# Square sums of the differential blocks moved out of the attention stage into the gate stage behind it

## The reference

```python
h, gate = _modulate(x, c, norm_g, w_ada, b_ada)
qa, ka, va, qb, kb, vb, g = _split(h @ w_in, EVEN_SPLITS)
...
ya = _window_gqa_sink(qa, ka, va, kac, vac, a_sink)
...
yb = _sweep_query_blocks(lambda n, qn: _diff_attend(qn, kb_all, vb_all, lam), qb)
yb = rmsnorm(yb, b_subln_g) * (1.0 - lam_init)
y = jnp.concatenate([ya.reshape(B, S, -1), yb.reshape(B, S, -1)], axis=-1) * jax.nn.silu(g)
x = x + gate * (y @ w_out)
```

## Time and profile before

| | |
|---|---|
| median of three runs | 2830.58 us (2827.45 to 2832.51) |
| the profiled execution | 2830.81 us, of which its span 2829.0 us |
| PE busy | 2726.1 us, 96% |
| DVE busy | 1069.9 us, 38% |
| ACT busy | 785.7 us, 28% |
| POOL busy | 223.7 us, 8% |
| differential stage | about 560 to 770 us |
| gate stages | about 769 to 917 us |

### The profile page before, as it was taken

How to read it: one execution, slowest core, us unless ns; L and a number is a source line. 1 busy time by engine, 2 the same in 40 slices (tenths; PEclk the granted TensorE clock), 3 DMA queues, 4 the chain that set the end, 5 groups by cost and what they waited for, 6 DMA issues and landing times. The chain is left out here.

```text
span 2829.0 us, 32445 instructions
## 1 busy us (share of the span) xinstructions
PE 2726.1 (96%) x12154; PEld 1529.1 (54%) x12154; DVE 1069.9 (38%) x3023; ACT 785.7 (28%) x1684; POOL 223.7 (8%) x409
## 2 busy tenths in 40 slices
PE   5999999999999999999999999999999999999998
PEld 3477544477644445466745476444654465644443
DVE  3257521299712223344400174123833473212211
ACT  3136400277711112322200264112211462111100
POOL 2000000000000000000060030200000002012000
PEclk8999999999999999999999999999999999999999
DMA  7030000012011220211010001333220204134311
GB/s 261 7 109 32 20 30 30 30 68 72 34 65 65 79 86 19 93 38 38 12 54 30 30 22 42 86 83 119 96 71 30 71 16 133 67 119 168 133 60 45
DMA packets 71867, 188.46 MB, mean 67 GB/s; under 512 B 6844, under 2 KB 9600, under 8 KB 70784
## 3 DMA queue, kind: packets, MB, share of 16 engines
q0 software_dynamic: 27808, 99.04, 10.8%
q1 hardware_dynamic: 43152, 86.97, 8.9%
q10 hardware_dynamic: 752, 0.38, 0.0%
HBM read 143.69 MB, written 43.01 MB: 66 GB/s over the span
## 5 line engine op out<-in xcount | busy, mean ns | idle before, releaser
L1305 PE MATMUL psum<-RW,hT 128*128 128x512 f32 (+2 forms) x2208 | 926.2, 575 | 7.5 <-ACT hT L2197 4.7
L1305 PEld LDWEIGHTS psum<-RW,hT 128*128 128x128 f32 x2208 | 428.0, 198 | 434.8 <-issue 412.8
L1271 PE MATMUL psum<-RW,RQ 128*128 128x512 f32 x832 | 362.3, 594 | 1.1 <-ACT RQ L2234 1.1
L1341 PE MATMUL psum<-RQ 64*128 64x256 f32 (+5 forms) x1344 | 291.7, 492 | 2.3 <-DVE small L2038 1.5
L2383 ACT ACTIVATE RP<-RP,small 128x1280 f32<-128x1280 f32 (+11 forms) x274 | 252.0, 920 | 131.0 <-DVE small L2038 127.0
L2038 DVE CUSTOM_DVE_ANT_0 RP<-psum,small 128x512 f32<-128x512 f32 (+1 forms) x382 | 201.5, 574 | 178.5 <-PE psum L1341 89.7
L1271 PEld LDWEIGHTS psum<-RW,RQ 128*128 128x128 f32 x832 | 157.0, 191 | 191.4 <-issue 191.4
L1353 PE MATMUL psum<-ident,RP 128*128 128x128 f32 x1388 | 203.7, 281 | 9.8 <-DVE RP L2051 4.5
L2395 ACT ACTIVATE RP<-psum 128x512 f32<-128x512 f32 (+1 forms) x288 | 150.1, 521 | 192.0 <-PE psum L1353 180.3
L1353 PEld LDWEIGHTS psum<-ident,RP 128*128 128x128 f32 x1388 | 149.4, 141 | 81.7 <-issue 67.9
L1341 PEld LDWEIGHTS psum<-RQ 64*128 64x128 f32 (+1 forms) x1344 | 139.2, 186 | 90.4 <-issue 48.9
(11 more groups left out here) (321 smaller groups left out, 2284.3 us busy)
## 6 DMA issues: line engine op xcount, KB each, us to landing
RW<-in_w_in SPq DMA_DIRECT2D x7, 2048.0 KB, 8.1
RW<-in_ev_w_in SPq DMA_DIRECT2D x6, 2048.0 KB, 8.1
RW<-in_od_w_ada SPq DMA_DIRECT2D x6, 2048.0 KB, 7.9
RW<-in_od_w_in SPq DMA_DIRECT2D x5, 2048.0 KB, 7.9
RQ<-in_ev_w_ada SPq DMA_DIRECT2D x4, 2048.0 KB, 21.0
RX<-in_x POOLq DMA_DIRECT2D x16, 512.0 KB, 6.0
y_even<-YR POOLq DMA_DIRECT2D x20, 256.0 KB, 2.3
RP<-y_even POOLq DMA_DIRECT2D x20, 256.0 KB, 3.0
```

The lines of the kernel that those rows point to most:

```text
L1271: last = pe.matmul(main.bank(f), yT[:, kk, :], w_buf(n)[:, kk, :], start=kk == 0, stop=kk == KC - 1)
L1305: last = pe.matmul(main.bank(f)[:, 0:nc_], lhs_of(st["lhs"], j["t"], kk), w, start=kk == 0, stop=kk == kn - 1)
L1341: last = pe.matmul(main.bank(f)[:, 0:pc["w"]], q, kk[:, keys], start=i == 0, stop=i == len(u["qk"]) - 1)
```

## The change

The square sums are no longer formed pair by pair in the differential stage. In the first gate stage POOL first loads all ten differential blocks (ten transfers of 128 by 512) into `RP`, columns 2048 to 7167, and then its own y slices as before. DVE forms the 40 square sums from there, those of two tiles behind its product of each of the tiles 3 to 7. ACT's Ln and Exp stand at the end of the first gate stage, with a table load ahead of them. The second gate stage reads its y from the loaded blocks, so its ten loads are gone.

```diff
+        s_diff_y = sem("diff_blocks_loaded")
...
-                             y=(y_even, 512 * j), gain=(None, "subln")[j]) for j in range(2)]
+                             y=((y_even, 0), None)[j], gain=(None, "subln")[j]) for j in range(2)]
+        gate_even = stages[-2:]
...
+        diff_y = RP[:, 2048:7168].rearrange("p (t c) -> p t c", t=NTC)
...
                 elif k == "gate":
-                    for j in st["tiles"]:
+                    if st is gate_even[0]:
+                        for t in with_ctx:
+                            gp.dma_start(diff_y[:, t, :], y_even[t * P:(t + 1) * P, 512:1024]).then_inc(s_diff_y, 16)
+                    for j in st["tiles"] if st["y"] else ():
...
+            def diff_squares(t):
+
+                dve.wait_ge(s_diff_y, 16 * NTC)
+                fence()
+                for h in range(4):
+                    y = diff_y[:, t, P * h:P * h + P]
+                    ins = dve.tensor_tensor_reduce(temp[:, P * h:P * h + P], y, y, 1.0 / 128, 0.0, ALU.mult, ALU.add,
+                                                   diff_norm[:, 4 * t + h:4 * t + h + 1])
+                    sig(ins, s_sq if 4 * t + h == 39 else s_dve)
...
                             if st["gain"] is None:
+                                dve.wait_ge(s_yload[y_g[0] % 4], 16 * (y_g[0] // 4 + 1))
+                                y = RP[:, 512 * (y_g[0] % 4):512 * (y_g[0] % 4) + 512]
+                                y_g[0] += 1
                                 sig(tt(so, so, y, ALU.mult), s_stage)
+                                if st is gate_even[0] and 3 <= t < 8:
+                                    diff_squares(2 * t - 6)
+                                    diff_squares(2 * t - 5)
                             else:
                                 dve.wait_ge(s_rstd, att_diff["pairs"][-1]["rq"] + 1)
                                 for h in range(4):
                                     hs = slice(P * h, P * h + P)
-                                    last = stt(so[:, hs], y[:, hs], diff_norm[:, 4 * t + h:4 * t + h + 1], so[:, hs],
+                                    last = stt(so[:, hs], diff_y[:, t, hs], diff_norm[:, 4 * t + h:4 * t + h + 1], so[:, hs],
                                                ALU.mult, ALU.mult)
...
-                        if k == "diff":
-                            dve.wait_ge(s_ot, u["g"] + 1)
-                            y = pair_block(st, u["block"])[:, u["y"]:u["y"] + P]
-                            i = u["hp"]
-                            n = 4 * u["t"] + i
-                            ins = dve.tensor_tensor_reduce(temp[:, P * i:P * i + P], y, y, 1.0 / 128, 0.0, ALU.mult, ALU.add,
-                                                           diff_norm[:, n:n + 1])
-                            sig(ins, s_sq if u["rq"] is not None else s_dve)
-                            return
...
-                            if i:
-                                pair_y(ps[i - 1])
...
-                        pair_y(ps[-1])
...
+                    if st is gate_even[0]:
+                        act.preload_act_table_set("natural_log_exp_and_others")
+                        act.wait_ge(s_sq, sq_index[att_diff["pairs"][-1]["rq"]])
+                        step(fn(diff_norm, diff_norm, ACT.Ln, bias=epsc))
+                        fn(diff_norm, diff_norm, ACT.Exp, scale=-0.5).then_inc(s_rstd, 1)
...
-                        act.wait_ge(s_sq, sq_index[ps[-1]["rq"]])
-                        step(fn(diff_norm, diff_norm, ACT.Ln, bias=epsc))
-                        fn(diff_norm, diff_norm, ACT.Exp, scale=-0.5).then_inc(s_rstd, 1)
```

More of the change, by code:

```diff
@@ L741, in build @@
         PROJ = ("rope", "kv_window", "copy", "gate", "latent_in", "rope_part", "qknorm", "ssm_in")
-        y_stage_of = [j["st"] for s in stages if s["kind"] == "gate" for j in s["tiles"]]
+        y_stage_of = [j["st"] for s in stages if s["kind"] == "gate" and s["y"] for j in s["tiles"]]
+        diff_y = RP[:, 2048:7168].rearrange("p (t c) -> p t c", t=NTC)
         def stored_until(stage):
@@ L1931, in _ @@
                             main.wait_drained(dve, f)
-                            dve.wait_ge(s_yload[y_g[0] % 4], 16 * (y_g[0] // 4 + 1))
-                            y = RP[:, 512 * (y_g[0] % 4):512 * (y_g[0] % 4) + 512]
-                            y_g[0] += 1
                             if st["gain"] is None:
+                                dve.wait_ge(s_yload[y_g[0] % 4], 16 * (y_g[0] // 4 + 1))
+                                y = RP[:, 512 * (y_g[0] % 4):512 * (y_g[0] % 4) + 512]
+                                y_g[0] += 1
                                 sig(tt(so, so, y, ALU.mult), s_stage)
+                                if st is gate_even[0] and 3 <= t < 8:
+                                    diff_squares(2 * t - 6)
+                                    diff_squares(2 * t - 5)
                             else:
```

## The result

| | before | changed |
|---|---|---|
| median, 7 runs each | 2830.91 us (2827.45 to 2833.19) | 2838.97 us (2831.83 to 2840.64) |
| ratio, 95% interval | | 1.0022 (1.0012 to 1.0032) |
| profiled execution | 2830.81 us, span 2829.0 | 2831.83 us, span 2830.0 |
| mean granted clock of the 7 runs | | 0.9906; 0.992 in the profiled one |

The forecast was 2832.0 us with a range up to 2836.5. Timed again with 11 runs against 35 of the kernel before, the changed kernel stood at 2836.39 against 2832.96 us, ratio 1.0014 (1.0006 to 1.0023): some 0.1 to 0.3% slower is what can be said. A single profile is therefore not enough here, and the trace of it looks at first like the forecast come true.

The account below looks back on a forecast made before the run. PE, busy 96% of the span, was taken as the bound. The terms -0.8 + 2.0 = +1.2 us on the profiled 2830.81 us gave 2832.0 us, range 2827.5 to 2836.5.

Parts of the forecast that it names:

- Square sums leave the differential stage: Differential stage: 0.12 us gained in each of about seven pairs of 256 keys, 0.8 us; nothing in pairs of 1280 keys.
- rows 4: Differential stage, pairs of 1280 keys: the first minimum starts when PE's scores are there, so removing square sums gains nothing.
- Ten loads ahead of the first slice: Start of the first gate stage: first y slice lands at 784.2, wanted by 782.2, so PE waits 2.0 us, once.
- The wait costs its own length: First gate stage: PE's wait for the first y slice entered the sum as +2.0 us, ends 0 and 4.2 us.
- Squares, tables, x loads: Gate stages and output stage loads: squares in tiles 3 to 7, table loads and earlier x loads are hidden, 0 us each.

Follow-up runs that it names:

- e2: The changed kernel, but POOL issues the first four y slices ahead of the ten differential blocks; median 2830.99 us, ratio 0.9996 to the kernel before.
- e7: The changed kernel, but only the first y slice is issued ahead of the ten differential blocks; median 2832.72 us, ratio 1.0000 to the kernel before.
- e3: The kernel before, with the ten loads added ahead of its first y slice and square sums left in the differential stage; median 2838.81 us, ratio 1.0021.
- e5: The kernel before, with ten idle DVE instructions ahead of its multiply of tile 0 in the first gate stage, no load added; median 2837.17 us, ratio 1.0016.
- e4: The changed kernel, with 20 transposes of the identity ahead of the transposes of tile 0 in the first gate stage; median 2836.23 us.
- e1: The changed kernel with no edit, timed again and profiled in another execution; median 2836.39 us.

## Why the prediction was wrong, step by step

- *Square sums leave the differential stage: -0.8 us.* Right, in size and in every trace of a kernel that has it (-0.79 to -0.81). But it is made up differently, and that the sum came out is in part luck. I had 0.12 us in each of about seven pairs of 256 keys. The trace has about 0.2 us in two of them (1.60 us a round and not 1.68) and none in the round between, 0.4 us in all. The other 0.4 us came from within the pairs of 1280 keys, which I had put at nothing: the kernel before has two pairs in which the scores take 2.81 and 2.82 us in place of 2.45, the changed kernel one. By my own sign ("if they got shorter, my reading of rows 4 is wrong") that reading was too broad; it held for the regular pairs, which kept their 0.84 us.
- *Ten loads ahead of the first slice: PE waits 2.0 us.* Right in mechanism, and nearly in size: 2.2 to 2.5 us. Landings 0.73 us apart, continued from four loads, put the slice within 0.6 us of where it landed, by two errors that nearly cancel: the first load landed 3.1 us after its issue and not 3.9, and the landings then came 0.87 us apart. The fit that the Trainium skill's page "DMA: Bandwidth & Descriptors" gives in its section "Anatomy of one DMA — SWDGE (gpsimd) path" for one DMA, taken for the eleven as one stream, made an estimated 8.6 us. It was further off than the rows: the trace shows 11.8 us.
- *The wait costs its own length.* This is the step that failed: the term "PE then waits 2.0 us, once" stands in the sum as +2.0. I priced 2.0 us of idle PE as 2.0 us of time. In three of four profiles the clock fell to 0.50 behind it, which brought the stage's loss to an average of (2.6 + 4.1 + 4.4 + 4.4) / 4 = 3.9 us. I had taken the clock from the page's row of tenths, where it is full in all but the first slice, and asked no further. The trace before had evidence against it: PE's wait of 2.04 us at 1136.78, and the window that follows it,

```profile
1136.78 0.66 PE L1150 MATMUL psum<-ident,RS 128*128 128x128 f32 x4 [2.04 <-DVE RS L1981]
```

```profile
1137.60:1141.00 3.40, 2.89 (x4) 1.37 (x5) 0.00 (x0) 0.41 (x2) 0.00 (x0) 0.50 0.09 36
```

  A wait of two us with half clock behind it was there to be read. It should have put a second price beside the first: in the same trace two waits of 2.0 us, at 63.99 and 1136.78, have half clock behind them, and two others, 2.63 us at 1121.57 and 2.33 us at 2685.75, have not. With 1.5 to 1.8 us for such a stretch, and half of the waits, an estimate from these rows adds about 0.8 us on average and 1.8 at the top. In the kernel before one stretch of half clock stands between 1098 and 1157 us; in all four profiles of the changed kernel that part is 1.6 to 1.9 us longer, with clock 0.92 over 1120 to 1165 us in place of 0.96. The first line is the kernel before, the second the changed one:

```profile
1120.00:1165.00 45.00, 39.21 (x122) 20.73 (x122) 17.23 (x58) 9.41 (x29) 0.00 (x0) 0.96 0.09 30
```

```profile
1120.00:1165.00 45.00, 40.45 (x122) 21.00 (x120) 16.64 (x54) 7.96 (x23) 0.00 (x0) 0.92 0.11 30
```

- *Squares, tables, x loads: 0 us each.* Right; e2 has the squares, the tables and the moved loads, and its gate stages are as long as before. In the changed kernel ACT's two table loads stand at 840.38 and 842.29 and were done 3.5 us before the next tile's end.
- *The range.* The account by stretches is -0.8 + 3.9 + (2.7 - 1.4) = 4.4 us, the last term being the mean of the two right-hand columns, changed less before. Measured over all 18 runs of the changed kernel and the 42 of before that stood beside them, the means differ by 2837.6 - 2832.8 = 4.8 +- 0.7 us. The first result's 8 us is a difference of medians; its means differ by 7.1 +- 1.4 us. I take the rest as the luck of seven runs, since eleven more gave 4.1 +- 0.8, but nothing shows it separately. My range leant on three runs of before and on one execution's trace; the spread of before over 35 runs is 2827.79 to 2838.55 us.

What stays open is first the 1.3 us further on. Later stretches at 0.50 also differ among executions of the kernel before, and e2, which has no wait, lost 3.0 us between 1098 and 1157 us in its one profile where e7 lost 0.2. Whether the new wait has a part in these later stretches, beyond the one behind it, is not shown. The totals of e3 and e5 (+6.0 and +4.3), with full clock near 785 in their one profile each, are averages of runs that have no trace. That the lower clock follows the wait is shown, in three of four profiles of the changed kernel and in none of the five of kernels without a wait there (before, e2, e7). That it makes up most of the mean difference beyond the wait is argued from sums. That it is PE's idle time, and nothing else about the late slice, which lowers it is argued too: e4, which should have tested that, decides nothing, and e5's profile does not show the fall.

The version to keep is e2 (or e7): all of the change but the order of the loads. It has the 0.8 us in its trace, but these runs don't separate it from the kernel before (0.9996, 0.9988 to 1.0005).

## What to carry to other kernels

When a step is moved to "a stage with room", list what it puts ahead of the first thing that stage needs: ten loads cost nothing behind the first slice and several us in front of it. Price a new wait of PE by its length and by the clock that the trace shows behind waits of that length, not by its length alone; look at all such waits, since only a part of them has the lower clock behind it. And before a difference of a tenth of a per cent is believed, compare several executions by stretches between the same PE instructions: it separates a start that varies by 6 us from a change of 0.8.

## What the runs showed of the hardware

The granted clock fell to 0.50 (1.2 GHz) behind waits of PE of only 2.2 to 2.5 us in a program that otherwise kept PE busy, in three of four profiles of the changed kernel, and not behind the waits of 2.1 and 1.8 us in the one profile each of e3 and e5. The same wait of 2.63 us near 1121 us had the full clock behind it in the kernel before and half clock in e1. Around the end of a wait of 10.1 us it was at 0.50 for 10.2 us, in which PE worked for 5.2 us. Each stretch of 3.4 us at 0.50 right behind the wait near 785 us cost 1.5 to 1.8 us. Fourteen loads of 256 KB in a row on one queue were issued 0.53 us apart; the first ten landed 3.1 to 6.4 us after their issue, and the eleventh 6.5 us after, so that the landings fell behind the issues by about 0.3 us a load.
